# The first loads, turns and splits of a two-layer decoder: tile 0 of x and the identity first, four weight halves in one run, tile 1 turned inside the second panel, and constant products on TensorE

## The reference, cut to what matters

```
h = x @ w_in                      # x (256, 1024), w_in[l] (1024, 3088)
qa, ka, va, qb, kb, vb, qc, kc, vc, gc, rc = jnp.split(h, IN_BOUNDS[1:-1], axis=-1)
...
x = layer_norm(DEEPNORM_ALPHA * x + mix, ln_mix_g[l], ln_mix_b[l])
...
```

## Time and profile before

| | us |
|---|---|
| median of 3 runs | 1745.12 (1745.03 to 1745.25) |
| the profiled execution, its own time | 1744.54 |
| its span, first to last instruction | 1742.7 |
| PE busy with matmuls in the span | 1706.1 (98%) |
| DVE busy | 1329.2 (76%) |
| ACT busy | 1019.6 (59%) |

### The profile page before, as it was taken

The page is one execution under the profiler, slowest core; times in us unless marked ns, Lnnn a source line. Parts: engine busy times, 40 slices in busy tenths (PEclk is TensorE's granted clock), DMA queues, the critical chain, the costliest instruction groups (busy, mean ns, idle before and its releaser), DMA issues.

```text
span 1742.7 us, 21666 instructions
## 1 busy us (share of the span) xinstructions
PE 1706.1 (98%) x7978; PEld 1364.8 (78%) x7978; DVE 1329.2 (76%) x1226; ACT 1019.6 (59%) x901; POOL 22.1 (1%) x32
## 2 busy tenths in 40 slices
PE   7999999999999999899999999999999999999996
PEld 6856788888785578787888888888888888888885
DVE  4575756545566585689899898898898998998996
ACT  4354344434344444277677777777776776777774
POOL 0001000000000100000000000000000000000000
PEclk9999999999999999899999999999999999999998
DMA  8522436546463242789999999999999999999991
GB/s 301 194 76 76 166 122 212 174 150 231 153 231 105 97 162 104 264 302 355 338 372 371 341 362 370 343 365 353 355 364 357 350 366 339 361 378 338 363 369 64
DMA packets 206487, 465.98 MB, mean 267 GB/s; under 512 B 11968, under 2 KB 14560, under 8 KB 206432
## 3 DMA queue, kind: packets, MB, share of 16 engines
q1 hardware_dynamic: 200896, 463.76, 74.6%
q10 hardware_dynamic: 5536, 1.48, 0.4%
HBM read 464.16 MB, written 1.05 MB: 267 GB/s over the span
## 4 chain that ended last, share of the span: by engine, by line
PE 90%; DVE 6%; DMA 2%; ACT 2%; issue 1%; ACTq 0%; SPq 0%; DVEq 0%
PE ps L1578 20%; PE ps L2053 17%; PE ps L2055 17%; PE ps L2054 17%; PE ps L1606 5%; PE ps L1970 3%; PE ps L2030 2%; PE ps L2039 1%; PE ps L1535 1%; DVE w_lo L977 1%; PE ps L1890 1%; PE ps L1871 1%; DMA ring<-in_w_in_dram 1%; PE ps L1803 1%; PE ps L1734 1%
## 5 line engine op out<-in xcount | busy, mean ns | idle before, releaser
L977 DVE TENSOR_TENSOR w_lo<-ring,w_hi 128x2048 fp32r<-128x2048 f32 x336 | 768.0, 2290 | 112.4 <-ACT w_hi L633 109.4
L633 ACT CAST w_hi<-ring 128x2048 fp32r<-128x2048 f32 x336 | 642.0, 1911 | 277.0 <-PE ps L2055 263.4
L2053 PE MATMUL ps<-w_hi,xe_hi 128*128 128x512 f32 x896 | 353.1, 394 | 1.8 <-DVE w_lo L977 1.8
L2055 PE MATMUL ps<-w_hi,xe_lo 128*128 128x512 f32 x896 | 349.3, 390 | 0.0
L2054 PE MATMUL ps<-w_lo,xe_hi 128*128 128x512 f32 x896 | 348.6, 389 | 0.0
L1578 PE MATMUL ps<-ring_r,xT_r 128*128 128x512 f32 (+1 forms) x760 | 199.4, 392 | 2.8 <-DVE ring_r L965 1.3
L2053 PEld LDWEIGHTS ps<-w_hi,xe_hi 128*128 128x128 f32 x896 | 168.3, 188 | 37.1 <-DVE w_lo L977 2.8
L2055 PEld LDWEIGHTS ps<-w_hi,xe_lo 128*128 128x128 f32 x896 | 168.2, 188 | 35.7
L2054 PEld LDWEIGHTS ps<-w_lo,xe_hi 128*128 128x128 f32 x896 | 168.4, 188 | 33.7
L2053 PE MATMUL ps<-w_hi,he_hi 128*128 128x512 f32 x448 | 178.1, 397 | 0.0
L2055 PE MATMUL ps<-w_hi,he_lo 128*128 128x512 f32 x448 | 174.8, 390 | 0.0
(11 more groups left out here) (273 smaller groups left out, 1803.2 us busy)
## 6 DMA issues: line engine op xcount, KB each, us to landing
ring<-in_moe_w_dram SPq DMA_DIRECT2D x336, 1024.0 KB, 5.6
ring<-in_ffd_w_dram SPq DMA_DIRECT2D x31, 1024.0 KB, 5.1
ring<-in_w_in_dram SPq DMA_DIRECT2D x24, 1024.0 KB, 6.1
ring<-in_xa_wkv_dram SPq DMA_DIRECT2D x16, 1024.0 KB, 5.0
ring<-in_w_out_dram SPq DMA_DIRECT2D x8, 1024.0 KB, 5.0
ring<-in_xa_wq_dram SPq DMA_DIRECT2D x8, 1024.0 KB, 5.0
ring<-in_xa_wo_dram SPq DMA_DIRECT2D x8, 1024.0 KB, 5.2
ring<-in_ffd_w_dram SPq DMA_DIRECT2D x4, 512.0 KB, 3.6
```

The source lines that it names most:

```text
L633: act.copy(w_hi[:, q % SPLIT_SLOTS, :], ring[:, q % RAW_SLOTS, :]).then_inc(hi_ready, 1)
L977: dve.tensor_tensor(w_lo[:, q % SPLIT_SLOTS, :], ring[:, q % RAW_SLOTS, :], w_hi[:, q % SPLIT_SLOTS, :].bitcast(F32), ALU.subtract).then_i ...
L2053: pe.matmul(ps[:, bank, :], x_hi, hi[:, c, cols], start=first, stop=False)
L2055: return pe.matmul(ps[:, bank, :], x_lo, hi[:, c, cols], start=False, stop=last)
```

## The change

SP loads tile 0 of x and the identity alone, then halves 0 to 3, and then tile 1 of x, the rest of `square` (both on a new semaphore `x_rest`), the memory tokens and half 4. The bytes are the same. ACT and DVE split halves 0 to 3 in one run and split tile 1 behind them. PE turns tile 0, makes panel 0 and the first half of panel 1 for tile 0, waits for `x_rest`, turns tile 1, makes the second half of panel 1 for tile 0, and goes on with tile 1. POOL fills `above` (128x128, unused until the router of layer 1) with ones, and PE multiplies it by itself seven times before it waits for x, and nine times behind the turn of tile 0; the products go to a PSUM bank that the first matmul of panel 0 overwrites.

```diff
--- before.py
+++ after.py
@@ -350,6 +350,7 @@
         acc_init = sem("acc_init")
         out_done = sem("out_done")
         last_added, mean_ready = sem("last_added"), sem("mean_ready")
+        warm_set, x_rest = sem("warm_set"), sem("x_rest")
         vstep = sem("vstep")
         sstep = sem("sstep")
         pstep = sem("pstep")
@@ -459,8 +460,11 @@
 
         @block.sync
         def _(sp):
-            sp.dma_start(x[:, :, :], a["x"][0].rearrange("(t p) d -> p t d", p=P)).then_inc(x_in, 16)
-            sp.dma_start(square[:, :, :], a["square"]).then_inc(x_in, 16)
+            def load_x(t, signal):
+                sp.dma_start(x[:, t, :], a["x"][0].rearrange("(t p) d -> p t d", p=P)[:, t, :]).then_inc(signal, 16)
+
+            load_x(0, x_in)
+            sp.dma_start(square[:, 0, :], a["square"][:, 0, :]).then_inc(x_in, 16)
 
             def load_ln(k):
                 l, s = divmod(k, 3)
@@ -481,6 +485,8 @@
                 for n in range(L1 if l == 0 else MIX_PANELS):
                     dense(l, n)
                     if l == 0 and n == 1:
+                        load_x(1, x_rest)
+                        sp.dma_start(square[:, 1:4, :], a["square"][:, 1:4, :]).then_inc(x_rest, 16)
                         sp.dma_start(mem_tok, a["mem"][0].rearrange("(t p) d -> p t d", p=P)).then_inc(mem_in, 16)
                     if n == IN_P + KV_P + OUT_P - 1:
                         load_ln(3 * l)
@@ -532,6 +538,7 @@
 
         @block.gpsimd
         def _(pool):
+            pool.memset(above[:, 0, :, :, :], 1.0).then_inc(warm_set, 1)
             pool.memset(mhalf[:, :], -0.5).then_inc(pstep, 1)
             pool.memset(cpad[:, :, :, CK:64], 0.0).then_inc(pstep, 1)
             pool.wait_ge(pstep, 2)
@@ -632,9 +639,8 @@
                     act.wait_ge(half_used, ITEM_HALVES * i + (q + 1))
                 act.copy(w_hi[:, q % SPLIT_SLOTS, :], ring[:, q % RAW_SLOTS, :]).then_inc(hi_ready, 1)
 
-            split_high(2)
+            split_high(4)
             turn_split(TURN["x0"], (1,))
-            split_high(2)
             for dst, src in (
                 (mask_a[:, :, :], a["mask_a"]), (mask_b[:, :, :], a["mask_b"]), (level[:, :, :], a["level"]),
                 (lamv[:, :, 0, :], a["lam_q1"].unsqueeze(0).to_broadcast([P, DEPTH, AQ])),
@@ -978,9 +984,8 @@
                                   w_hi[:, q % SPLIT_SLOTS, :].bitcast(F32), ALU.subtract).then_inc(lo_ready, 1)
 
             turn_split(TURN["x0"], (0,))
-            split_low(2)
+            split_low(4)
             turn_split(TURN["x0"], (1,))
-            split_low(2)
 
             dve.wait_ge(pos_in, 32)
             done(dve.tensor_copy(pos[:, :], pos_i[:, :]))
@@ -1610,14 +1615,27 @@
                 if chunks[-1] == KC - 1:
                     ins.then_inc(kv_psum, 1)
 
+            pe.wait_ge(warm_set, 1)
+
+            def keep_warm(count):
+
+                warm = above[:, 0, :, :, :].rearrange("p t e f -> p (t e f)")
+                for _ in range(count):
+                    pe.matmul(ps[:, 0, 0:P], warm, warm, start=True, stop=True)
+
+            keep_warm(7)
             pe.wait_ge(x_in, 32)
-            for t in range(T):
-                turn_tile(TURN["x0"], x, t)
+            turn_tile(TURN["x0"], x, 0)
+            keep_warm(9)
 
             for l in range(DEPTH):
                 if l == 0:
                     turned(TURN["x0"], 0)
-                    gemm_pair(l, 0, 0)
+                    gemm(l, 0, (0,))
+                    gemm(l, 1, (0,), range(12))
+                    pe.wait_ge(x_rest, 32)
+                    turn_tile(TURN["x0"], x, 1)
+                    gemm(l, 1, (0,), range(12, STEPS))
                     turned(TURN["x0"], 1)
                 else:
                     turned(TURN["x3", l - 1], 0)
```

## The result

| | before | after |
|---|---|---|
| median, us (5 runs each) | 1745.03 (1744.14 to 1745.25) | 1753.60 (1753.26 to 1756.09) |
| the profiled execution, its own time | 1744.54 | 1753.60 |
| its span | 1742.7 | 1751.8 |
| PE takes up panel 2 (first matmul on qk_r) | 38.3 | 44.42 |
| end of its 192 matmuls | 82.99 | 91.74 |

The ratio is 1.0051 (95% interval 1.0040 to 1.0063): slower by 8.6 us, where +1.2 was forecast and 1748.3 was the upper end of the range. The whole difference is there by the end of panel 2.

What follows compares the result with a forecast made beforehand. The prediction took PE to bound the first 90 us, from 12.47 to 82.99. ACT's lateness 1.9 less 0.7 slack gave +1.2, so 1745.12 + 1.2 = 1746.3 us, range 1743.2 to 1748.3.

Steps and rivals of the forecast that it cites:

- The place and the kind of loss: Ahead of and inside half 4: PE's early start given back waiting for ACT, net +1.2 us; likeliest case, chance 0.61.
- The loads: Start of the kernel: half 0 lands 2.0 us earlier, at 8.4, with 1.5 as lower bound; first matmul near 10.4.
- The arrival at panel 2: PE reaches panel 2 at 37.2 (half clock) or 36.2 (full clock) instead of 38.3, a gain of 1.1 to 2.1.
- the lateness of the start alone: ACT's fourteen issues start 1.8 to 2.9 us later, carried to the last issue as 1.9; less 0.7 slack, +1.2.
- The term that failed: ACT's queue: the last of fourteen issues ends 0 to 2.9 us later, taken as 1.9; half 5's load changes nothing.
- slower for good: Rival, chance 0.06: half 5's load gets between ACT's issues, second w_rank waits 2.7 more; lateness 5.6, net +4.9, 1750.0.
- the clock's worth at the start: PE's first eight matmuls at half clock cost 1.6 us over full speed; the products could bring between nothing and 1.6.
- hole that I forecast myself: PE waits ahead of and inside half 4 for ACT's cast, after arriving at panel 2 at 37.2 or 36.2.
- the sum: Profiled execution 1742.7 + 1.2 + 1.84 = 1745.7; median 1745.12 + 1.2 = 1746.3.
- what it cites of the Trainium skill on transposes: PE's start: transposes don't count towards the full clock as matmuls do, so plain products could raise it.
- The products: PE's start: seven constant products take 1.2 to 1.6 us, nine take 1.6 to 2.1, all hidden in PE's waiting.
- The rule on issuing: ACT's queue: by the skill, initiating DMAs is usually small, giving -1.1 to -2.1; the trace disagrees with 13.8 us.

Runs made afterwards that it cites:

- e3: The kernel before, with ACT's fourteen issues waiting for DVE's low part of half 2; 1746.54 us, ratio 1.0006.
- e4: The changed kernel with SP's load of half 5 held back until the sine is done; 1748.61 us, a single execution.
- h1: The changed kernel with SP's load of half 5 held back until PE has released half 6's buffer; 1746.82 us, ratio 1.0009.
- g3: The kernel before with only ACT's fourteen issues moved to later places, as in g1; 1745.16 us, ratio 1.0000.
- f4: The kernel before, with ACT's fourteen issues waiting for DVE's low part of half 3; 1755.81 us, ratio 1.0060.
- g2: g1 without the sixteen constant products; 1745.06 us, ratio 1.0000.
- g1: The changed kernel, eleven ACT issues moved behind the memory tokens' copies, w_rank and w_router behind later casts, first users one panel later; 1744.26 us, ratio 0.9997.
- k2: g1 with fourteen constant products behind the turn of tile 0 instead of nine; 1743.28 us, ratio 0.9988.
- k1: The changed kernel with w_router and the two w_rank first among ACT's fourteen issues; 1751.28 us, ratio 1.0026.
- e2: The changed kernel with w_router and both w_rank issued later, behind the copies of the turned memory tokens; 1745.35 us, ratio 0.9999.

## Why the prediction was wrong

*Right.* The place and the kind of loss: the chain's first 90 us, PE's early start given back in front of half 4, waiting for the cast that stands behind ACT's fourteen issues. Panels behind 83 us carried the shift almost unchanged (0.35 of 9.1). The loads: half 0 came 1.5 earlier, which I had as the lower end (8.96, taken 8.4), and the first matmul followed at 11.03 for 10.4. The arrival at panel 2, 1.7 early, lies within the 1.1 to 2.1. The direction, slower, was right too, but by the lateness of the start alone, which makes 1.2 of the 8.6.

*The term that failed* is "the last issue therefore ends 0 to 2.9 us later; I take 1.9". It was 7.2. The start was as told (2.4 late, inside 1.8 to 2.9), and e3 shows that 2.3 of late start do carry through as 2.4. What failed is the sentence behind it: "The row of half 5's load, issued at 28.23 now and earlier then, falls into the same issues and gives no reason for less." I asked of that row only whether it gave less, never whether it gave more. The earlier trace rows show the load issued while w_rank was under way, and the closer look above shows the last of them begun 1.3 us ahead of it. The change moves ACT's issues 2.4 back and the load 1.7 forward: 4.1 us against a margin of 1.3 for the second w_rank and 1.9 for the first. The order had to turn over, and the two w_rank, which I had taken over at 6.03 or less, took 12.05.

*The rival that was right* is "slower for good", which had just this mechanism and got 0.06. Against it I put "SP issues its loads in 0.37 while ACT is blocked", which only shows that SP isn't the one blocked. Its price was also short: it let one w_rank wait for one half more (lateness 5.6) where both were stretched (about 0.6 to 4.12 and 5.39 to 7.90; lateness 7.2), and had no term for the clock, which fell in the hole and cost 2.6. Its 5.6 would have been a net 4.9; with the measured lateness the same rule gives 7.2 - 0.7 = 6.5, near the 6.1 measured at the start of panel 2.

*The clock at the hole.* I had the clock's worth at the start (1.6) but nothing for it at the hole that I forecast myself. The first four matmuls on qk_r show it in e3, in e4 and in h1:

```profile
39.63 1.17 PE L1579 MATMUL ps<-qk_r,xT_r 128*128 128x512 f32 x4 [1.86 <-ACT qk_r L614]
```

```profile
40.40 1.18 PE L1585 MATMUL ps<-qk_r,xT_r 128*128 128x512 f32 x4 [2.73 <-ACT qk_r L623]
```

```profile
41.77 1.82 PE L1585 MATMUL ps<-qk_r,xT_r 128*128 128x512 f32 x4 [3.91 <-ACT qk_r L623]
```

Behind holes of 1.86 and 2.73 they ran at full speed, behind 3.91 and 7.83 slowly, and the 192 took 46.47 and 47.32 instead of 44.68: 1.8 and 2.6 more. The hole that I forecast myself, 37.2 or 36.2 to 39.5, lay between these rows, and the sum should have carried 0 to 1.8 for it.

*The clock at the start.* The prediction let bear out what it cites of the Trainium skill on transposes: sixteen of them, and slow matmuls behind. Two executions of kernels whose PE does just the same up to there disagree. This is PE in e3:

```profile
7.74 3.67 PE L1536 MATMUL ps<-square,x 128*128 128x128 f32 x16 [7.74 <-DMA square<-in_square_dram]
12.51 1.17 PE L1579 MATMUL ps<-ring_r,xT_r 128*128 128x512 f32 x4 [1.09 <-ACT ring_r L614]
```

In e3 and g3 the first eight ran at full speed with no product ahead of them, in before and f4 slowly. So the full clock at the start of after is no proof that the products brought it. What they are worth stands in the medians: 0.8 from g2 to g1, 1.8 from g2 to k2, which has five more. And the 1.6 that I had for the eight slow matmuls was too much for the order of before: g3, with all of them fast, takes up panel 2 only 0.56 earlier (37.75 for 38.31), because PE then waits for the low parts of the halves.

*The products.* Each of them is two rows in the trace (seven are x14, nine x18), so seven cost 3.35 and nine 2.85 where I had 1.2 to 1.6 and 1.6 to 2.1: I divided the gather's time by its 32 rows, and these are 16 products. Both still lay in PE's waiting, so no time hung on it in the result; in k2 the size of this cover did.

*The rule on issuing.* In after ACT's sequencer spends 18.6 us on fourteen issues that carry 1.4 MB. The Trainium skill, DMA: Bandwidth & Descriptors, Issuing engines are not separate DMA queues, calls that time usually small, and says in the same place that DMAs of different engines interleave on the same 16 DMA engines; the trace disagrees with the first half and agrees with the second, 866 packets against 866 in 38 to 43 us. Its section Queues, rings and completion order has each DMA engine take turns between queues, a packet at a time, and means by a packet several descriptors; the equal counts agree if a turn takes equally many rows from either queue.

*Still open* is what holds ACT's sequencer. In after, from 26 to 32 us, the DMA engines are nearly idle (share 0.19, 48 GB/s) although half 5's load is issued at 26.52, and none of its packets moves in that time: queue 1 doesn't appear there. e4 has the same nearly idle stretch (0.09, 17 GB/s, from 29 to 32 us) with no load of a half on its way at all. So for five microseconds it isn't bandwidth that is short, nor is it half 5's load that keeps the DMA engines idle; from 32 us on the load of half 5 and its successors fill the DMA engines, and ACT's packets take turns with them. The runs show what stands behind what, not the mechanism in between.

## What to carry to other kernels

When two engines issue DMAs, write down the order in which their issues interleave and the margin at each neighbour, and see whether the change turns one over: here a margin of 1.3 us decided over some 7 us (h1), and durations read in the old order say nothing about the new one. Keep a run of small DMA issues away from an engine whose next piece of work somebody waits for; g1 and k2 did with a later place what the other order inside the run (k1) did not. And if a forecast has a hole in TensorE of several microseconds, it needs a term for the clock as well.

## What the runs showed of the hardware that I had not expected

- A DMA issue on ACT takes 0.35 to 0.5 us in a quiet stretch, up to 6.2 us with nothing but ACT's own constants on the queues (e4's second w_rank), and up to 8.1 us with loads of halves beside them (f4's second w_rank). Its own rows have little to do with it: two w_rank took 2.58 ahead of half 5's load (k1) and 12.05 behind it (after).
- The same works on the load: half 5's took 11.6 us to land in after and 10.70 in e2, against 5.0 in g1, where the constants weren't issued yet, and 5.1 in e4, where they were all but through. And on SP's own issuing: in h1 its load of half 6 took 3.29 us to issue, for the usual 0.37.
- Equal packet counts, 866 and 866, for 1.72 and 0.04 MB: small packets of one queue went one for one with large packets of the other.
- Right behind the products TensorE's first eight matmuls ran at full speed after a gap of at most 0.85 us (after, e2, k1, k2) and for the most part slowly after one of 2.24 to 2.55 (g1, h1, e4), where the granted clock fell only between 11 and 12 us, after they had begun. In front of panel 2, behind a long busy stretch, the clock stayed up over 1.86 (e3) and 2.73 (e4) and fell in or right behind gaps of 3.91 (h1) and 7.83 (after). So gaps of 2.2 to 2.7 went either way; what PE had done before them differed, and more the rows don't show.
- The same start doesn't always get the same clock: behind sixteen transposes and a gap of 1.08 to 1.34 us the first matmuls were slow in before and f4 and fast in e3 and g3.
